# Spare expert weights loaded behind the first two gathers, a bias table stored late, and a projection unit between attention steps

## The reference

```python
def first_block(x, ...):                  # 256 tokens of width 1024
    for i in range(2):
        u = rmsnorm(h, norm_mix[i])
        h = h + (dsw_mixer, moba_mixer)[i](u, ...)      # attention A (24 heads), attention B (16 heads)
        h = h + sq_relu_mlp(rmsnorm(h, norm_ffn[i]), ffn_w1[i], ffn_w2[i])

def second_block(x, c, ctx, ...):
    for i in range(2):                    # x and ctx in layer 0, x alone in layer 1
        mod = silu(c) @ mod_w[i] + mod_b[i]             # shifts, scales, gates
        x = x + g1 * mixer(modulate(rmsnorm(x)))        # attention with convolution / with pooling
        x = x + g2 * moe(modulate(rmsnorm(x)))          # 32 experts in 4 groups, top 2
```

## Time and profile before

| | us |
|---|---|
| median of 3 runs | 2326.96 (2321.44 to 2332.65) |
| the profiled execution, its own time | 2329.66 |
| its span | 2327.6 |
| TensorE busy (matmul) | 2093.2, 90% of the span |
| VectorE, ScalarE, GpSimd busy | 754.4, 379.6, 232.0 |
| mean granted clock of TensorE | 0.949 of full |
| DMA queue of SP, share of 16 engines | 63.5% |

### The profile page before, as it was taken

One profiled execution on the slowest core, in us unless ns is written; L12 is line 12 of the kernel. 1 busy time (PEld: TensorE's weight loads), 2 busy tenths in 40 slices (PEclk: granted clock), 3 DMA queues, 4 the chain that ended last, 5 costly groups with the idle time before them and its releaser, 6 DMA issues. The chain is left out here.

```text
span 2327.6 us, 22306 instructions
## 1 busy us (share of the span) xinstructions
PE 2093.2 (90%) x8740; PEld 1091.9 (47%) x8740; DVE 754.4 (32%) x1585; ACT 379.6 (16%) x811; POOL 232.0 (10%) x270
## 2 busy tenths in 40 slices
PE   8999999998999999899898899989488899899895
PEld 3456666444666657445433333334254433344332
DVE  2126774114677224874310111111433311111111
ACT  2132000114100021552100000000332100000000
POOL 2000000000000100330121111111000011111110
PEclk9999999999999999999799999989699799999998
DMA  9942888441588721103599999999653699999996
GB/s 255 325 140 73 298 298 294 159 143 63 174 304 302 266 73 73 73 19 127 214 397 411 395 416 372 403 412 423 264 209 122 235 414 423 421 413 371 414 419 250
DMA packets 129450, 631.59 MB, mean 271 GB/s; under 512 B 14886, under 2 KB 17094, under 8 KB 103008
## 3 DMA queue, kind: packets, MB, share of 16 engines
q1 hardware_dynamic: 108336, 579.29, 63.5%
q0 software_dynamic: 18048, 33.30, 5.2%
q10 hardware_dynamic: 2992, 18.02, 2.1%
HBM read 625.46 MB, written 26.57 MB: 280 GB/s over the span
## 5 line engine op out<-in xcount | busy, mean ns | idle before, releaser
L1098 PE MATMUL PS<-ring,arena 128*64 128x512 f32 x992 | 493.1, 655 | 90.4 <-DMA ring<-ex_up 88.7
L1101 PE MATMUL PS<-ring,arena 128*64 128x512 f32 x1008 | 500.9, 655 | 0.0
L1098 PEld LDWEIGHTS PS<-ring,arena 128*64 128x64 f32 x992 | 143.6, 150 | 374.6 <-issue 353.4
L465 PE MATMUL PS<-ring,arena 128*128 128x512 f32 (+1 forms) x736 | 298.9, 562 | 6.0 <-issue 3.6
L1427 DVE COPY arena<-PS 128x512 f32<-128x512 f32 x64 | 44.3, 692 | 639.1 <-PE PS L1088 639.1
L1116 PE MATMUL PS<-ring,arena 128*64 128x512 f32 x1008 | 231.5, 601 | 1.5 <-DVE arena L1423 1.5
L796 PE MATMUL PS<-arena,ring 128*128 128x256 f32 x1024 | 224.7, 380 | 3.3 <-DVE arena L416 1.7
L807 PE MATMUL PS<-ring,arena 128*128 128x512 f32 x512 | 222.2, 592 | 0.0
L796 PEld LDWEIGHTS PS<-arena,ring 128*128 128x128 f32 x1024 | 193.4, 190 | 39.5 <-issue 13.8
L465 PEld LDWEIGHTS PS<-ring,arena 128*128 128x128 f32 x736 | 138.6, 192 | 147.0 <-issue 141.0
L807 PEld LDWEIGHTS PS<-ring,arena 128*128 128x128 f32 x512 | 97.2, 190 | 116.0 <-issue 115.3
(11 more groups left out here) (264 smaller groups left out, 1861.2 us busy)
## 6 DMA issues: line engine op xcount, KB each, us to landing
ring<-ex_up SPq DMA_DIRECT2D x63, 2048.0 KB, 22.3
ring<-ex_down SPq DMA_DIRECT2D x63, 2048.0 KB, 23.0
ring<-ex_gate SPq DMA_DIRECT2D x62, 2048.0 KB, 17.1
ring<-ffn_w SPq DMA_DIRECT2D x32, 2048.0 KB, 12.8
ring<-mod_w SPq DMA_DIRECT2D x24, 2048.0 KB, 8.1
ring<-a_w_qkv SPq DMA_DIRECT2D x9, 2048.0 KB, 29.6
ring<-b_w_qkv SPq DMA_DIRECT2D x6, 2048.0 KB, 9.2
ring<-w_in_ab SPq DMA_DIRECT2D x3, 2048.0 KB, 8.1
```

What stands on the lines that cost most here:

```text
L465: mm = pe.matmul(PS[:, u % 4, 0:w.width], q.src[:, k, w.t * P:(w.t + 1) * P], w8(w.tile, w.width)[:, k, :], start=(k == 0), stop=(k == KD ...
L1098: g = pe.matmul(PS[0:CAP, u, :], xT[:, k, :], gate[k], start=(k == 0), stop=(k == KD - 1))
L1101: h = pe.matmul(PS[CAP:P, u, :], xT[:, k, :], up[k], start=(k == 0), stop=(k == KD - 1))
```

## The change

Three parts.

1. `proj_stage` gets a table of banks, and unit 0 of `pr_b` gets bank 6, which attention B gives up: its turned probabilities now take banks 4 and 5 in turn, and a turning waits until the copy of the step two before is made. Term p of unit 0 is issued in the hook of `pe_pairs` behind the scores of step 2p+3, after a wait for the output of step 2p. `pe_proj` does units 1 to 3.
2. `bias_b` is stored behind the last `bias_load_a`; the first loads of `bias_a` wait for `bias_a` alone, and `bias_load_b` for both.
3. ScalarE issues `down_a` and the second piece of `gate_b` behind a wait for the first two gathers. All spare pieces of a stage share one semaphore, and each reader waits for all of them.

The diff, without its unchanged parts:

```diff
@@ -720,7 +720,7 @@
-        def proj_stage(src, units, ready, temp=None):
+        def proj_stage(src, units, ready, temp=None, bank=lambda u: u % 8):
             n = len(units)
...
@@ -731,17 +731,19 @@
                     w.done = (s.product, b.product + products)
-            return Record(src=src, units=units, s=s, b=b, ready=ready, done=[(s.added, b.added + n)],
+            return Record(src=src, units=units, s=s, b=b, ready=ready, done=[(s.added, b.added + n)], bank=bank,
                            temp=temp if temp is not None else xn[:, :, 0:BANK])
-        def pe_proj(pe, x):
+        def pe_proj(pe, x, first=0):
             at(pe, *x.ready)
             for u, w in enumerate(x.units):
+                if u < first:
+                    continue
                 tile_full(pe, w.tile)
...
                 for i, (k, rhs) in enumerate(w.terms):
-                    mm = pe.matmul(PS[:, u % 8, :], x.src(k)[:, w.t * P:(w.t + 1) * P], rhs,
+                    mm = pe.matmul(PS[:, x.bank(u), :], x.src(k)[:, w.t * P:(w.t + 1) * P], rhs,
                                    start=(i == 0), stop=(i == len(w.terms) - 1))
...
@@ -762,7 +764,7 @@
                 at(dve, w.done)
-                src = PS[:, u % 8, :]
+                src = PS[:, x.bank(u), :]
                 if w.gate is not None:
...
@@ -1007,12 +1009,12 @@
             q_b.done, lambda i, u: area(W0 + 512 * (i % 2) + 256 * u, 256)[:, 0:P * (i % 2 + 1)],
-            [area(W0 + 1024, BANK), area(W0 + 1536, BANK)], lambda j: 4 + j % 3, lambda i, u: 2 * (i % 2) + u, 2, 7)
-        at_b.turned_free = lambda j, bank: at_b.copies_to[j - 2] if j >= 3 else 0
+            [area(W0 + 1024, BANK), area(W0 + 1536, BANK)], lambda j: 4 + j % 2, lambda i, u: 2 * (i % 2) + u, 2, 7)
+        at_b.turned_free = lambda j, bank: at_b.copies_to[j - 1] if j >= 2 else 0
         pr_b = proj_stage(lambda k: ot_b[:, k, :], [
...
                     res=hx[:, t, h * BANK:(h + 1) * BANK], gate=None) for h in range(2) for t in range(2)],
-            at_b.done)
+            at_b.done, bank=lambda u: u if u else 6)
         n_b2 = norm_stage(hx, XL, vcol("norm_ffn", 8, 8), None, pr_b.done)
...
@@ -1213,7 +1215,6 @@
                 act.dma_start(tokens_d[t * P:(t + 1) * P, :], row).then_inc(s.token_stored[t % 2], 16)
-            spare_load(act, m, "down_a", 0)
             act.wait_ge(s.group_top, b0.group_top + 1)
...
@@ -1222,7 +1223,8 @@
             for u in range(2):
-                act.wait_ge(s.token_stored[u], b0.token_stored0 + 16 * (T // 2))
+                act.wait_ge(s.gathered[u], b0.gathered0 + 16)
+            spare_load(act, m, "down_a", 0)
             spare_load(act, m, "gate_b", 1)
...
@@ -1736,19 +1738,16 @@
                               weighted=tiles, weights_ready=1, spare_used=3 + l,
-                              **{f"spare_{part}": 16 * len(pieces) for part, pieces in spare_pieces[l].items()},
-                              **({} if l else {"spare_gate_a": 0}))
+                              spare_loaded=16 * sum(len(pieces) for pieces in spare_pieces[l].values()))
             m.o = sems(f"over{l}", "full down_full down gathered step y_stored")
             m.done = [(m.s.combined, m.b.combined + tiles)]
-            sem_of = dict(down_a=m.s.spare_down_a, gate_b=m.s.spare_gate_b, up_b=m.s.spare_up_b, gate_a=m.s.spare_gate_a)
-            base_of = dict(down_a=m.b.spare_down_a, gate_b=m.b.spare_gate_b, up_b=m.b.spare_up_b,
-                           gate_a=m.b.spare_gate_a)
+            all_loaded = m.b.spare_loaded + 16 * sum(len(pieces) for pieces in spare_pieces[l].values())
             m.spare = {}
...
                 m.spare[part] = Record(slot=None, pieces=pieces, columns=columns, rows=pieces[0][0],
-                                       loaded=sem_of[part], loaded_at=base_of[part] + 16 * len(pieces),
+                                       loaded=m.s.spare_loaded, loaded_at=all_loaded,
                                        done=m.s.spare_used, done_at=m.b.spare_used + n + 1)
...
@@ -1993,8 +1992,14 @@
             pe_qkv(pe, q_b)
-            pe_pairs(pe, at_b)
-            pe_proj(pe, pr_b)
+
+            def first_unit(slot):
+                p = (slot - 6) // 4
+                if slot >= 6 and slot % 4 == 2 and p < KD:
+                    pe.wait_ge(at_b.s.out, at_b.b.out + 2 * p + 1)
+                    pe_proj_part(pe, pr_b, 0, p, p + 1)
+            pe_pairs(pe, at_b, between=first_unit)
+            pe_proj(pe, pr_b, first=1)
             pe_awake(pe, 5, 3)
...
@@ -2389,10 +2394,12 @@
-            for rows, dst in ((browA, bias_a), (browB, bias_b)):
+            def bias_store(rows, dst):
                 src = bass.AP(tensor=rows.tensor, offset=rows.offset + P - 1,
...
                 pool.dma_start(dst, src).then_inc(s_bd, 16)
+
+            bias_store(browA, bias_a)
...
@@ -2403,7 +2410,7 @@
-            pool.wait_ge(s_bd, 32)
+            pool.wait_ge(s_bd, 16)
             at(pool, *n_a1.done)
...
@@ -2411,6 +2418,7 @@
             bias_load_a(3)
+            bias_store(browB, bias_b)
...
@@ -2421,6 +2429,7 @@
             pool.dma_start(convrows, ins["conv_w_2"][0]).then_inc(s_conv.w_rows, 16)
+            pool.wait_ge(s_bd, 32)
             at(pool, *n_b1.done)
...
```

## The result

The changed kernel takes 2310.34 us, median of 6 runs (2307.2 to 2321.15); the kernel before, in the same set, 2333.22 (2321.44 to 2341.9, 6 runs). The ratio is 0.9903, 95% interval 0.988 to 0.9926: 22.6 us less, 17 to 28. A second set of 6 runs gave 2309.74 and 0.9909 (0.9877 to 0.9941). The forecast was 2309.9, as -17.1 against an execution of 2329.66. The end point was met to 0.4 us, the difference was larger by some 5: the three runs shown with the kernel before had a median of 2326.96, all six of this set 2333.22. So the closeness of the end point is in part luck.

What follows compares the result with a forecast made beforehand. Full DMA engines in the expert stages were taken as the bound, with TensorE waiting for weight tiles. Terms -6.6 - 0.8 - 4.4 - 2.1 - 3.2 = -17.1 took 2329.66 to 2312.6, or 2309.9 from the median; range 2301 to 2320.

Steps and rivals of the forecast that it cites:

- Part 1, -6.6: Second attention: a projection unit moved between its steps saves 6.6 us, bounds -4.1 and -6.9.
- the last piece: Last iteration of the second attention: the final projection piece has little around it and costs 0.3 us.
- VectorE's slack of 1.0 us: Second attention: VectorE takes up scores 1.0 us late, so a piece costs nothing while that slack is there.
- Rival (b): Second attention: each piece costs its full 0.86 us, part 1 is zero, total -10.5, 2316.5 us; chance 0.08.
- Part 2, -0.8: Start of kernel: storing bias_b late removes TensorE's wait for its fourth weight tile; -0.8 us, bounds 0 and -0.8.
- The cover at the new place: Near 158 us: idle DMA engines take the late bias_b store at no cost; otherwise 2 MB or 5 us of transfer.
- Part 3, -9.7: Both expert stages: spare tiles behind the first gathers give -4.4 and -2.1 from gathers, -3.2 from the clock.
- The gathers: Expert stages: first gathers land sooner without spare loads, so tokens turn 4.4 us earlier in the first, 2.1 in the second.
- The clock term: First expert of both stages: full instead of half clock would save 6.3 us, counted half at -3.2, bounds 0 and -6.3.
- Rival (a): Expert stages: gathers are no faster, only parts 1 and 2 count, -7.4, 2319.6 us; chance 0.12.
- Rival (d): Expert stages: the spare loads' tail holds the refill, half of part 3 is kept, -12.2, 2314.8 us; chance 0.10.

Runs made afterwards that it cites:

- part 2 alone: Only the late store of bias_b, on the kernel before: 2330.39 us, ratio 0.9979 (0.9962 to 0.9997).
- part 1 alone: Only the projection unit issued between the steps of attention B, on the kernel before: 2325.98 us, ratio 0.997 (0.995 to 0.999).
- one more store: The kernel before with a third early 2 MB bias table store, the bias loads waiting for all three: 2349.23 us, ratio 1.0053.
- part 3 alone: Only the spare tiles issued behind the first two gathers, on the kernel before: 2329.8 us, ratio 0.9972 (0.9951 to 0.9992).
- five warming places: Changed kernel plus warming matmuls before both router products, in the norm behind expert stage 1 and at two attention heads: 2302.68 us, ratio 0.9876.

## Why the prediction was right, and where not

**Part 1, -6.6.** Right in mechanism, near in size: -7.0 (-11.7 to -2.3) in the runs. Five traces without it have B at 64.6 to 67.4 (mean 66.0), seven with it at 59.2 to 60.3 (mean 59.9): -6.1. Between the two profiled executions it is -4.5: the tail gives 6.9 (27.73 to 20.87), the steady pieces take 0.03 each, the last piece takes 0.2 (I had 0.3), and 2.0 go in the head, where the first piece meets half clock (2.08 us in place of 1.12). In the means the head takes 1.0 and the tail gives 7.4, since in two of the five traces the first microseconds of the projection ran partly at half clock (0.69 and 0.67 in the first 4 us). The head is a cost that I had at nothing. And the limit was another: I named VectorE's slack of 1.0 us; TensorE's own idle time of 0.8 comes first. Rival (b) was one piece away.

**Part 2, -0.8.** This term was mis-sized: -4.9 (-8.9 to -0.7) in the runs, -7.4 by stretch S in the traces (mean 138.9 with the early store, 131.5 with part 2 alone). The step was "so -0.8, bounds 0 and -0.8": the upper bound was the wait as one execution had it, and that wait is between 0.8 and 10.6 us from one execution to the next, with the half clock behind it on top. That the DMA engines were full at 144 GB/s around it was in my own text, and it should have set the bound: a transfer that far from its rate and that near to its deadline need not have a fixed wait. The cover at the new place was also mis-sized, as told above, without effect.

**Part 3, -9.7.** Right in mechanism and near in size. From the table, M1 falls from a mean of 700.1 (before, part 1 alone, part 2 alone, one more store) to 694.1 (part 3 alone and the two changed traces, which lie 10 us apart), M2 from 503.4 to 501.3: -8.1, and -6.5 (-11.4 to -1.9) in the runs. By place it is closer. The gathers: I had -4.4 and -2.1; from gather to turn it is 7.4 to 8.0 down to 2.9 to 3.05 (-4.7), and 6.7 to 7.0 down to 3.8 to 4.45 (-2.8). The clock term, counted half at -3.2, can be read from the turn to the first refill in the same traces: in stage 1 it falls from 12.0 to 12.4 us to 9.3, 9.3 and 11.0 (-2.3 in the mean), in stage 2 from 11.3 to 12.1 to 11.0 each time (-0.6). So it came to -2.9, most of it in stage 1. In the first changed trace the clock is full at 1123 to 1126 and falls behind the turning, and four pairs come at 0.85 us (seven before); in the second it holds there. In stage 2 it fell in both, and in part 3 alone. Two stretches of the first trace, a slow pair of it in each stage, then a pair of the second trace in stage 1:

```profile
1123.00:1126.00 3.00, 2.54 (x12) 1.50 (x10) 0.42 (x1) 0.00 (x0) 0.36 (x1) 1.00 0.16 48
1127.00:1129.00 2.00, 2.00 (x8) 0.61 (x6) 1.78 (x9) 0.53 (x1) 0.24 (x1) 0.50 0.74 319
```

```profile
1127.17 1.06 PE L1100 MATMUL PS<-ring,arena 128*64 128x512 f32 x1
...
1826.17 1.06 PE L1100 MATMUL PS<-ring,arena 128*64 128x512 f32 x1
```

```profile
1119.68 0.59 PE L1100 MATMUL PS<-ring,arena 128*64 128x512 f32 x1
```

That the 3 MB fit into the idle stretch is shown, with the loss of 12 us in the runs, 16 in the trace, where they don't. The three gains by place are -10.4 in all; why only 6.5 to 8.1 of it reach the end is open, and the spread of the runs would hide it.

**The order of issue, and the clock.** With ex_down issued early the runs lose 10 us, since what it delayed was needed at once and it was not. The rule to issue a DMA early and to wait on its semaphore late (the Trainium skill, "DMA: Bandwidth & Descriptors", Rules for kernel authors) would have left ex_down there. The same rule is right once the idle stretch is over: later still costs 12 us by the runs. The clock is at half where TensorE has stood still for microseconds: with 6 warming matmuls, which end 4.6 us before the turn in the earlier trace rows, seven pairs come at 0.85, with 16, which leave 0.16 us, all come at 0.43. That agrees with the half clock after an idle window (the Trainium skill, "TensorE: Matmul & The Clock Gate", The HAM clock gate). That state alone does not account for the first changed trace at 1126, nor for stage 2 of both: the clock fell there with no idle time behind the warming matmuls but the 0.78 us for VectorE's copy. What brings it down there is open.

**The sum.** -6.1, about -5 and -8.1 are 19; the runs say 22.6 and 21.2, and the 2 to 4 us between are inside their intervals. Rival (a) falls with the gathers. Rival (d) falls with the refill: it is issued 14.06 and 12.39 us behind the gather in the two changed traces, 5.9 and 7.5 earlier, and the tail of the spare loads holds it little: in the second one the first ring tile takes 9.0 us to land, 8.3 before. The forecast was right on its end point with one term too small by 4 us and a starting median 6 us too low; that the two cancelled is luck.

## What to carry to other kernels

A small latency-bound transfer on which a stage waits (here the first gather) should be issued with the DMA engines free; a bulk load that is due much later goes right behind it, if an idle stretch long enough follows, and no later. How long the bulk load holds a small transfer up is not its bytes at the full rate: here 2 MB issued 4.0 us ahead kept the gather until the bulk load itself had landed. When work is put into gaps, look first at the idle time of the engine that gets the work; its consumers' slack is only the second limit. A wait seen in one execution next to a saturated transfer is a draw, not a size: take two or three traces before it is used as a bound.

## What the runs showed that I had not expected

- The diagonal stores of the bias tables keep the DMA engines at 0.9 to 1.0 busy and 135 to 210 GB/s beside the weight loads, and at 97 GB/s where one runs nearly alone. The last of them lands 27.9 us behind its issue (one store), 51.4 (two) and 71.2 (three). TensorE's wait for the weight tile beside them is up to 10 us longer in one execution than in another.
- A mean busy share of 0.06 to 0.09 does not say that the DMA engines are free for a transfer: with ex_down early one of sixteen was still at work from 1118 to 1121, and the gather landed with it, at 1121.5.
- Where TensorE stood still for 9 to 19 us, the next 16 instructions took 2 to 2.7 us more.
- Executions of one kernel differ by 11 to 26 us, in part through half-clock spells in the light stretches, which come in one execution and not in another; five warming places took the mean granted clock of the span from 0.946 and 0.952 to 0.966.
